# A two-stage ConvFFN: openings, stage change and round changes rewritten

## The chip, the core and the metric

One core of a Trainium2 chip runs the whole program. TensorE (PE) multiplies and writes to PSUM, VectorE (DVE) and ScalarE (ACT) work on PSUM and SBUF, GpSimd (POOL) on SBUF alone, and SyncE (SP) issues nearly all DMAs. Each engine takes its instructions in order from its own queue and waits on semaphores that others raise. The metric is the device time of one launch in microseconds, the median of the runs.

## The reference, cut to what matters

A two-layer trunk (D = 1024, hidden size 3072) for a prompt of 1024 tokens and 64 sample tokens, 1088 columns in all. Every layer has a mixer and, after it, a gated ConvFFN. The change touches the two ConvFFNs alone:

```
def conv_ffn(xn, buf, w_g, w_u, w_c, b_c, w_d):
    g = xn @ w_g
    gc, new_buf = causal_dwconv(g, buf, w_c, b_c)       # 3 taps over the tokens
    return (jax.nn.gelu(gc) * (xn @ w_u)) @ w_d, new_buf
# in the layer: y = y + conv_ffn(rmsnorm(y, g_ffn[l]), ...)
```

## The kernel before

Activations lie as feature rows by token columns: `x_residual` has 8 tiles of 128 features by 1088 columns. Products are of fp32 values split in two: a *high* part (a rounded copy, by ScalarE) and a *low* part (value minus high, by VectorE or GpSimd), and three matmuls stand for one: high by high, low weight by high, high weight by low (L2151). The third of them, which alone reads the lows of the tokens, is the last third of a product (L2144).

The ConvFFN (class `Ffn`, L1843) uses a seven-product block scheme on halves of depth, features and tokens. A **job** is seven products, numbers 0 to 6: B21, B11, T1, T2, B22, NT4, T3 (L1839). T1, T2, NT4 and T3 are sums of half tiles of the tokens; S1 to S4 are sums of weights, made by VectorE in PSUM. Three pairs of PSUM banks, d, a and bb, take the products in turn (`GROUPS`, L1848); some products add into a pair or overwrite it, and what it held must have been read first. In the first stage a product is 24 matmuls of 272 columns, in the second 18.

First stage: 24 jobs (`JOBS1`) in 12 pairs of a gate and an up job. ScalarE copies products 0, 2, 3 and 5 out (`copy_out`), VectorE adds 1, 4 and 6 (`add_out`). In each pair the gate is scaled by the root of the squares (`scale_gate`), convolved (`conv_first` on ScalarE, `conv_tap` and `conv_samples` on VectorE), put through gelu, scaled again by GpSimd (`gate_scale`) and multiplied with up (`hidden_tile`); its four sums are made (`hidden_sum`) and SyncE stores it to DRAM. Second stage: 16 jobs in four **rounds** of four. In a round a quarter of the hidden features, seven *pieces* fetched from DRAM to staging buffers and made high by `piece_hi` and low by `piece_lo`, is multiplied with four groups of weights, and VectorE adds each product to the residual (`add_residual`). The residual was spilled to DRAM for the first stage and is fetched back (`reload`).

The order on each engine is written out by hand: `opening` (PE), `opening_act`, `open_dve` and `opening_dve` for job 0; then the loops in `tensor`, `scalar`, `vector`, `gpsimd` and `sync`; `down_first` is VectorE's order in the second stage's first job. The norm is applied late: GpSimd sums the squares of the tiles (L1661), a product with ones sums over features (L1669), ScalarE makes Ln and Exp of it (L1676, L1679), all inside job 0. Residual tiles 6 and 7 come last out of the mixer's output projection (`Output`, L1747), whose evacuations (L1828) stand in VectorE's queue among the opening's first steps.

In a round's first job TensorE waits before each product for the piece's low:

```
                    if m % QUARTERS == 0:
                        pe.wait_ge(*self.x_lo_done(m // QUARTERS, i))
```

## Time and profile before

| | us |
|---|---|
| median of 3 runs | 2579.86 (2578.29 to 2581.73) |
| profiled execution, its time | 2576.1 |
| its span | 2574.4 |
| first opening, first product to job 2's product 3 | 637.6 to 705.7 |
| second opening, the same | 1758.2 to 1828.9 |
| stage changes: the second stage's first two jobs | 1158.8 to 1205.9, 2282.0 to 2329.5 |
| round changes | three in each ConvFFN, the first at 1238 |

In a row of a timeline the first number is the start in us from the span's start, the second the length; then engine, line of the kernel, operation, what is written and read, shape, and the number of instructions merged. In brackets stands how long the engine was idle before it, and who ended that. Matmuls overlap, so the row of a product is a little longer than its share.

### The profile page before, as it was taken

The numbers are of one execution on the slowest core, as the hardware profiler recorded it, in microseconds if no ns is written. First come the engines' busy times: TensorE is split into PE (matmuls) and PEld (weight loads), VectorE is DVE, ScalarE is ACT, GpSimd is POOL, SyncE is SP. The second block draws the span as 40 slices with busy tenths as digits, with TensorE's granted clock in tenths as the row PEclk, the third lists the DMA queues.
The fourth block names the chain that finished last, engine by engine and source line by source line (L and its number), as shares of the span: only waits on it lengthen the run. The fifth ranks groups of instructions, "written<-read, shape, count | busy, mean of one in ns | idle before, by whom it ended". The sixth has DMA issues, their size and how long they took to land.

```text
span 2574.4 us, 46180 instructions
## 1 busy us (share of the span) xinstructions
PE 2466.7 (96%) x18693; PEld 2364.2 (92%) x18693; DVE 1765.6 (69%) x2158; ACT 1148.4 (45%) x1851; POOL 961.9 (37%) x623
## 2 busy tenths in 40 slices
PE   8999998899899999998999999998999999989998
PEld 7888886689899999998999999998999999989998
DVE  7466557645877777777778444637878777787775
ACT  5565756533544444442334433424444444443331
POOL 3234333214445454542223411343545454532221
PEclk9999999999999999999999999998999999999999
DMA  5101106752222232336443211222232222265422
GB/s 183 52 27 51 44 26 217 262 190 77 88 98 103 89 111 80 111 113 243 140 141 93 56 40 37 58 68 90 92 110 86 106 93 98 90 232 199 139 89 82
DMA packets 214178, 276.99 MB, mean 108 GB/s; under 512 B 11438, under 2 KB 158999, under 8 KB 210895
## 3 DMA queue, kind: packets, MB, share of 16 engines
q1 hardware_dynamic: 212910, 271.83, 31.7%
q8 instruction: 149, 2.44, 0.4%
q10 hardware_dynamic: 576, 2.10, 0.2%
q14 instruction: 63, 0.51, 0.1%
q0 software_dynamic: 480, 0.11, 0.0%
HBM read 203.57 MB, written 70.43 MB: 106 GB/s over the span
## 4 chain that ended last, share of the span: by engine, by line
PE 64%; DVE 9%; issue 3%; ACT 1%; POOL 1%; DMA 1%; SPq 0%; DVEq 0%; ACTq 0%; POOLq 0%
PE psum_all L2153 52%; PE psum_all L2810 7%; PE psum_all L148 3%; DVE down_x_ffn L2106 2%; DVE psum_all L2091 1%; DVE x_residual L2519 1%; DVE x_residual L2470 1%; DMA w_raw<-in_w_gate_dram 1%; PE psum_all L2862 0%; PE psum_all L2826 0%; POOL rms_scale L1661 0%; DVE blocks_down L2095 0%; POOL w_lo_part L113 0%; DVE ffn_x_sums L2407 0%; PE psum_all L2850 0%
## 5 line engine op out<-in xcount | busy, mean ns | idle before, releaser
L2153 PE MATMUL psum_all<-ffn_x,blocks 128*128 128x272 f32 x5760 | 737.6, 289 | 22.6 <-DVE ffn_x L2416 13.8
L2153 PEld LDWEIGHTS psum_all<-ffn_x,blocks 128*128 128x128 f32 x5760 | 731.0, 190 | 24.3 <-issue 15.7
L2153 PE MATMUL psum_all<-down_x_ffn,blocks_down 128*128 128x272 f32 x2880 | 376.9, 292 | 24.4 <-DVE x_residual L2519 11.5
L2153 PEld LDWEIGHTS psum_all<-down_x_ffn,blocks_down 128*128 128x128 f32 x2880 | 370.3, 191 | 28.7 <-issue 27.9
L2268 ACT COPY x_residual<-psum_all 128x544 f32<-128x544 f32 x192 | 117.9, 614 | 374.7 <-PE psum_all L2153 371.3
L113 POOL TENSOR_TENSOR w_lo_part<-w_raw,w_hi_part 128x1024 fp32r<-128x1024 f32 x52 | 126.8, 2439 | 355.9 <-ACT w_hi_part L97 355.8
L2519 DVE TENSOR_TENSOR x_residual<-x_residual,psum_all 128x544 f32<-128x544 f32 (+1 forms) x224 | 178.4, 797 | 114.2 <-PE psum_all L2153 112.7
L2470 DVE SCALAR_TENSOR_TENSOR x_residual<-x_residual,ffn_params 128x1088 f32<-128x1088 f32 x96 | 215.2, 2242 | 0.0
L2101 POOL TENSOR_TENSOR x_residual<-x_residual,rms_scale 128x1088 f32<-128x1088 f32 x48 | 153.2, 3191 | 151.7 <-ACT x_residual L2297 151.7
L2455 DVE TENSOR_TENSOR x_residual<-x_residual,psum_all 128x544 f32<-128x544 f32 x144 | 130.1, 904 | 93.2 <-PE psum_all L2153 91.3
L2095 DVE TENSOR_TENSOR blocks<-psum_all,blocks 128x512 fp32r<-128x512 f32 x144 | 99.2, 689 | 121.8 <-ACT blocks L2249 121.8
L2810 PE MATMUL psum_all<-operand_a,w_hi_part 128*128 128x364 f32 (+1 forms) x672 | 170.0, 331 | 0.0
L909 PE MATMUL psum_all<-in_hi_even,w_hi_part 128*128 128x384 f32 (+1 forms) x456 | 157.0, 344 | 1.1 <-DVE xb_padded L1430 0.6
L1363 POOL TENSOR_TENSOR take_then_weights<-take_then_weights,x_residual 128x511 f32<-128x511 f32 (+3 forms) x96 | 94.9, 999 | 158.0 <-DVE x_residual L1395 119.1
L2153 PE MATMUL psum_all<-ffn_x,block_a 128*128 128x272 f32 x1152 | 152.0, 288 | 1.3 <-ACT rms_scale L1676 1.3
L2153 PE MATMUL psum_all<-ffn_x,block_s 128*128 128x272 f32 x1152 | 151.8, 287 | 0.0
L909 PE MATMUL psum_all<-in_lo_even,w_hi_part 128*128 128x384 f32 (+1 forms) x456 | 149.3, 327 | 0.0
L2153 PEld LDWEIGHTS psum_all<-ffn_x,block_a 128*128 128x128 f32 x1152 | 146.9, 188 | 2.4 <-issue 2.4
L909 PE MATMUL psum_all<-in_hi_even,w_lo_part 128*128 128x384 f32 (+1 forms) x456 | 149.1, 327 | 0.0
L2153 PEld LDWEIGHTS psum_all<-ffn_x,block_s 128*128 128x128 f32 x1152 | 147.0, 188 | 0.0
L1395 DVE TENSOR_TENSOR_SCAN x_residual<-x_residual,all_ones 128x512 f32<-128x512 f32 (+3 forms) x96 | 91.8, 990 | 73.1 <-ACT x_residual L1183 73.1
L2500 POOL TENSOR_TENSOR x_residual<-x_residual 128x544 f32<-128x544 f32 x88 | 130.1, 1479 | 6.3
(361 smaller groups left out, 4630.1 us busy)
## 6 DMA issues: line engine op xcount, KB each, us to landing
staging_ffn<-hidden_spill SPq DMA_DIRECT2D x54, 816.0 KB, 5.2
hidden_spill<-x_residual SPq DMA_DIRECT2D x24, 1088.0 KB, 4.0
w_raw<-in_w_gate_dram SPq DMA_DIRECT2D x24, 1024.0 KB, 5.4
x_residual<-in_w_up_dram SPq DMA_DIRECT2D x24, 1024.0 KB, 5.2
pages<-in_cache_k_dram SPq DMA_DIRECT2D x64, 256.0 KB, 3.7
pages<-in_cache_v_dram SPq DMA_DIRECT2D x64, 256.0 KB, 4.6
x_spill<-x_residual SPq DMA_DIRECT2D x24, 546.0 KB, 5.4
x_residual<-x_spill SPq DMA_DIRECT2D x24, 546.0 KB, 5.8
```

The lines of the kernel that those rows point to most:

```text
L113: pool.tensor_tensor(dst if dst is not None else self.lo[:, par, :], self.raw[:, par, :], (hi if hi is not None else self.hi[:, par, :]).b ...
L909: mm = pe.matmul(bank(key, 0, b - a), wt[:, n % 2, col], xt[:, k, a:b], start=k == 0 and s == 0, stop=k == KT - 1 and s == 2)
L1363: pool.tensor_tensor(t[:, 0:n - 1], t[:, 0:n - 1], k[:, 1:n], ALU.mult).then_inc(weighted, 1)
L2095: eng.tensor_tensor(self.block(n, i, 1).rearrange("p (q c) -> p q c", c=P), self.source(n, i), self.block(n, i, 0).bitcast(F32).rearrange( ...
L2101: pool.tensor_tensor(self.conv[:, r, :], self.conv[:, r, :], self.core.rb[:, 0:USED], ALU.mult).then_inc(self.gr_ready, 1)
L2153: mm = pe.matmul(self.core.ps[:, b + h, 0:HB], wt[:, q * P:(q + 1) * P], xt[:, q, HB * h:HB * (h + 1)], start=first and at == 0, stop=at = ...
L2268: act.copy(self.half(self.target(n, r), h).rearrange("p (h n) -> p h n", h=2), self.group(name)).then_inc(self.act_out, 1)
L2455: dve.tensor_tensor(dst, dst, src, ALU.add).then_inc(self.dve_out, 1)
L2470: o.did(dve.scalar_tensor_tensor(gc, gb[:, j:j + USED], par[:, f + FT * j:f + FT * j + 1], gc, ALU.mult, ALU.add))
L2500: eng.tensor_tensor(dst, x, y, op).then_inc(self.hsum, 1)
L2519: dve.tensor_tensor(dst, dst, src, ALU.add).then_inc(self.dve_out, 1)
L2810: mm = pe.matmul(self.core.ps[:, self.lane_bank(f), 0:width(c)], wm[:, is_u, col], xm[:, k, chunk(c)], start=k == 0 and s == 0, stop=k == ...
```

## The change

All of it is in `Ffn` and in what calls it:

- Opening: TensorE's order in job 0 is 1, 2, 0, 4, 3, 5, 6 (it was 1, 0, 2, 3, 4, 5, 6). Each of the four token sums has one low, whole, by VectorE (`sum_lo`); GpSimd made half of two of them. TensorE waits for such a low at the product's last third (`made_first`). VectorE evacuates tile 6 behind S1 and S2 alone, the other first weights come after it.
- The squares of tiles 6 and 7 go to another scratch (`late_sq`), so that the high of block 4 waits for less. Squares are addressed as two halves. GpSimd's last addition of squares, the sums over features, Ln and Exp come in job 1.
- VectorE's order in job 1 is `first_pair_dve`. The last steps of the first pair (gelu 1, both gate scalings, `hidden_tile(0)`, the hidden sums) come in job 2.
- Spill and reload share one semaphore for each pair of tiles, and waits ask for the pair that they need.
- Stage change: ScalarE makes the highs of two pieces behind product 4 of job 23, of one behind each of 5 and 6, of three in job 24 (all seven came in job 23); the last gelu comes behind the copy of product 5, GpSimd's last gate scaling in job 24; VectorE has a new order in `down_first`; in the first ConvFFN SyncE asks for piece 4 ahead of the reload.
- Round changes: TensorE waits for a piece's high before the product and for its low at its last third. T1's low moves on VectorE from behind product 4's add to behind product 5's.
- The transposes of the state rows stand behind product 3 of job 25, not 2.

```
+    FIRST_PIECES = {(-1, 4): (B21, B11), (-1, 5): (T1,), (-1, 6): (T2,), (0, 1): (NT4,), (0, 2): (T3,)}
...
-                if up and i in (3, 5):
+                if n == 0 and i == 1:
+                    self.add_squares(pool, KT - 1)
+                if up and n > 1 and (i == 3 or i == 5 and n < JOBS1 - 1):
                     self.gate_scale(pool, t, (i - 3) // 2)
-                if up and i == 6 and n < JOBS1 - 1:
-                    self.hidden_sum(pool, t, T1)
-                if n and n % 2 == 0 and n < JOBS1 and i == 0:
+                elif n == JOBS1 and i == 1:
+                    self.gate_scale(pool, PAIRS - 1, 1)
+                elif n == 2 and i in (0, 1):
+                    self.gate_scale(pool, 0, i)
+                if up and i == 6 and 1 < n < JOBS1 - 1 or n == 2 and i == 1:
+                    self.hidden_sum(pool, (n - 1) // 2, T1)
+                if n and n % 2 == 0 and n < JOBS1 and i == (1 if n == 2 else 0):
                     for k in (T3, T2, NT4):
                         self.hidden_sum(pool, t - 1, k)
             if behind and n >= JOBS - QUARTERS:
                 behind(n - (JOBS - QUARTERS))
...
+            if x_low and (q, s) == (0, 2):
+                x_low()
...
     def opening(self, pe):
+        def made_first(i):
+            pe.wait_ge(*self.lo_ready(0, i))
+            pe.wait_ge(self.act_lead, self.T_HI[i])
+            self.multiply(pe, 0, i, lambda: pe.wait_ge(self.lead_lo, self.T_LO[i]))
         pe.wait_ge(self.out.evac, KT - 1)
         pe.wait_ge(self.b_lo, 10)
         pe.wait_ge(*self.lo_ready(0, 1))
         self.multiply(pe, 0, 1)
-
-        def tile_ready(q):
-            if q == 3:
-                pe.wait_ge(self.b_lo, 11)
-
         pe.wait_ge(self.out.evac, KT)
-        self.multiply(pe, 0, 0, tile_ready)
-        pe.wait_ge(*self.lo_ready(0, 2))
-        pe.wait_ge(self.t1_lo, 2)
-        self.multiply(pe, 0, 2)
-        pe.wait_ge(*self.lo_ready(0, 3))
-        pe.wait_ge(self.t2_lo, 1)
+        made_first(T1)
+        pe.wait_ge(self.b_lo, 11)
+        pe.wait_ge(*self.lo_ready(0, 0))
+        self.multiply(pe, 0, 0)
+        pe.wait_ge(self.b_lo, 12)
+        pe.wait_ge(*self.lo_ready(0, 4))
+        pe.wait_ge(self.act_out, 1)
+        self.multiply(pe, 0, 4)
         pe.wait_ge(self.dve_out, 1)
-        self.multiply(pe, 0, 3)
-        pe.wait_ge(self.act_out, 1)
-        self.sums_pe(pe, (0, 1))
-        pe.wait_ge(*self.lo_ready(0, 4))
-        pe.wait_ge(self.b_lo, 12)
+        made_first(T2)
         pe.wait_ge(self.act_out, 2)
-        self.multiply(pe, 0, 4)
-        self.sums_pe(pe, (2,))
-        pe.wait_ge(*self.lo_ready(0, 5))
-        pe.wait_ge(self.t2_lo, 2)
-        pe.wait_ge(self.s_root, 3)
-        self.multiply(pe, 0, 5)
-        pe.wait_ge(*self.lo_ready(0, 6))
-        pe.wait_ge(self.t3_lo, 2)
+        made_first(NT4)
         pe.wait_ge(self.act_out, 3)
-        self.multiply(pe, 0, 6)
+        made_first(T3)
 
     def tensor(self, pe, before=None, behind=None):
...
                     if m % QUARTERS == 0:
-                        pe.wait_ge(*self.x_lo_done(m // QUARTERS, i))
+                        pe.wait_ge(self.x_hi, 7 * (m // QUARTERS) + i + 1)
...
+                low = None
+                if m >= 0 and m % QUARTERS == 0:
+                    low = lambda: pe.wait_ge(*self.x_lo_done(m // QUARTERS, i))
+                self.multiply(pe, n, i, low)
+                if n == 1 and i == 1:
+                    pe.wait_ge(self.act_out, 5)
+                    self.sums_pe(pe, (0, 1))
+                elif n == 1 and i == 3:
+                    self.sums_pe(pe, (2,))
+                if m == 1 and i == 3:
                     pe.wait_ge(self.dve_out, dve + 1)
                     self.turn_state_rows(pe)
...
     def opening_act(self, act):
...
+        for i in range(3):
+        self.tile_hi(act, KT - 2)
+        self.block_hi(act, 0, 3)
+            self.even_copy(act, T1, q, 0)
+        act.wait_ge(self.s_sum, KT - 3)
+        self.block_hi(act, 0, 4)
+        self.even_copy(act, T3, 0, 1)
+        self.even_copy(act, T3, 1, 1)
+        self.sum_hi(act, T1)
+        self.even_copy(act, T3, 2, 1)
+        self.even_copy(act, T3, 3, 1)
+        self.square(act, KT - 2)
+        self.tile_hi(act, KT - 1)
+        self.square(act, KT - 1)
+        self.copy_out(act, 0, 2)
+        self.sum_hi(act, T2)
+        self.sum_hi(act, NT4)
+        self.sum_hi(act, T3)
+        self.block_hi(act, 1, 0)
+        self.block_hi(act, 1, 1)
+        self.copy_out(act, 0, 5)
+        for i in range(2, 7):
...
+    def first_conv_act(self, act, i):
+        if i == 1:
+            self.roots_act(act, (0, 1))
+        elif i == 3:
+            self.roots_act(act, (2,))
+            self.conv_first(act, 0, 0)
+            self.conv_first(act, 0, 1)
+        elif i == 6:
+            self.gelu(act, 0, 0)
...
+                if (n, i) == (JOBS1, 0):
+                    self.piece_hi(act, 0, B22)
...
+                elif (n, i) == (2, 0):
+                    self.gelu(act, 0, 1)
+                elif n == JOBS1 - 1 and i == 3:
+                    self.gelu(act, t, 0)
+                if n in (JOBS1 - 1, JOBS1):
+                    for k in self.FIRST_PIECES.get((n - JOBS1, i), ()):
+                        self.piece_hi(act, 0, k)
                 elif n >= JOBS1 and p == QUARTERS - 1 and r < ROUNDS - 1:
                     self.piece_hi(act, r + 1, i)
-                if m == 1 and i == 2:
+                if (n, i) == (JOBS1 - 1, 5):
+                    self.gelu(act, t, 1)
+                if m == 1 and i == 3:
...
+    def sum_lo(self, dve, i):
+        dve.wait_ge(self.act_lead, self.T_HI[i])
+        if i != T1:
+            dve.wait_ge(self.sum_lead, self.T_MADE[NT4][3])
+        dve.tensor_tensor(self.operand(0, i, 1), self.temp(i), self.operand(0, i, 0).bitcast(F32), ALU.subtract
+                          ).then_inc(self.lead_lo, 1)
...
+    def open_dve(self, dve):
+        self.tile_dve(dve, KT - 2)
+            self.t1_sum(dve, q)
+        self.t3_sum(dve, 0)
+        self.t3_sum(dve, 1)
+        self.t2_sum(dve, 0)
+        self.block_lo(dve, 0, 4)
+        self.sum_lo(dve, T1)
+    def opening_dve(self, dve):
+        self.nt4_sum(dve, 0)
+        self.tile_lo(dve, KT - 1, 0, B21, 0)
+        self.t3_sum(dve, 2)
+        self.t3_sum(dve, 3)
+        self.tile_lo(dve, KT - 1, 1, B22, 1)
+        for q in (1, 2, 3):
+        for q in (1, 2, 3):
+            self.nt4_sum(dve, q)
+        self.sum_lo(dve, T2)
+        self.sum_lo(dve, NT4)
+        self.add_out(dve, 0, 4)
+        self.sum_lo(dve, T3)
+        self.add_out(dve, 0, 6)
+    def first_pair_dve(self, dve, o):
+        self.block_lo(dve, 1, 4)
+        self.add_out(dve, 1, 1)
+        self.block_lo(dve, 1, 6)
+        self.block_sum(dve, 2, "S1")
+        self.block_sum(dve, 2, "S2")
+        self.block_lo(dve, 2, 2)
+        self.block_sum(dve, 2, "S4")
+        self.block_lo(dve, 2, 3)
+        self.block_sum(dve, 2, "S3")
+        self.scale_dve(dve)
+        self.scale_gate(dve, 0, 0)
+        self.scale_gate(dve, 0, 1)
+        self.conv_tap(dve, o, 0, 0, 1)
+        self.add_out(dve, 1, 4)
+        self.conv_tap(dve, o, 0, 0, 0)
+        self.conv_samples(dve, o, 0, 0)
+        self.block_lo(dve, 2, 4)
+        self.conv_tap(dve, o, 0, 1, 1)
+        self.conv_tap(dve, o, 0, 1, 0)
+        self.conv_samples(dve, o, 0, 1)
+        self.add_out(dve, 1, 6)
+        self.block_lo(dve, 2, 6)
...
+            self.block_sum(dve, u, "S1")
+            self.block_sum(dve, u, "S2")
+            if t == 1:
+                self.hidden_tile(dve, 0, 0)
+            self.hidden_tile(dve, t - 1, 1)
+            self.add_out(dve, g, 1)
+            self.block_lo(dve, u, 2)
+            self.block_sum(dve, u, "S4")
...
-                if turn and i == 4:
+                if turn and i == 5:
                     self.piece_lo(dve, r + 1, T1)
...
         self.piece_lo(dve, 0, T1)
+        self.block_lo(dve, n, 6)
         self.add_residual(dve, n, 0)
+        self.piece_lo(dve, 0, T2)
         self.add_residual(dve, n, 1)
-        self.piece_lo(dve, 0, T2)
+        self.next_sums(dve, n + 1)
         self.piece_lo(dve, 0, B22)
         self.add_residual(dve, n, 2)
+        self.next_lo(dve, n + 1, 2)
         self.piece_lo(dve, 0, NT4)
         self.add_residual(dve, n, 3)
+        self.next_lo(dve, n + 1, 3)
         self.piece_lo(dve, 0, T3)
-        self.next_sums(dve, n + 1)
-        self.next_lo(dve, n + 1, 2)
         self.add_residual(dve, n, 4)
-        self.next_lo(dve, n + 1, 3)
         self.add_residual(dve, n, 5)
         self.next_lo(dve, n + 1, 4)
```

## Rows read from the trace of the kernel before

**Rows 1.** The profile's page, busy time of each engine

```profile
PE 2466.7 (96%) x18693; PEld 2364.2 (92%) x18693; DVE 1765.6 (69%) x2158; ACT 1148.4 (45%) x1851; POOL 961.9 (37%) x623
```

**Rows 2.** Who TensorE waited for: us in total, times, longest us

```profile
PE psum_all L2153 <- DVE ffn_x L2416: 13.8, 2, 8.2
...
PE psum_all L2153 <- DVE x_residual L2519: 11.5, 8, 3.6
...
PE psum_all L2153 <- DVE down_x_ffn L2106: 9.4, 10, 4.0
```

**Rows 3.** Timeline of TensorE, opening of the first ConvFFN

```profile
637.60 3.18 PE L2153 MATMUL psum_all<-ffn_x,blocks 128*128 128x272 f32 x24
...
643.47 6.40 PE L2153 MATMUL psum_all<-ffn_x,blocks 128*128 128x272 f32 x48 [2.69 <-DVE x_residual L1828]
...
658.09 5.47 PE L2153 MATMUL psum_all<-ffn_x,blocks 128*128 128x272 f32 x24 [8.23 <-DVE ffn_x L2416]
...
699.69 12.24 PE L2153 MATMUL psum_all<-ffn_x,blocks 128*128 128x272 f32 x96 [0.41 <-DVE x_residual L2455]
```

**Rows 4.** Windows: length, busy us of five queues, TensorE's granted clock, DMA share, GB/s

```profile
658.00:660.00 2.00, 1.91 (x8) 1.94 (x9) 2.00 (x3) 1.17 (x1) 0.75 (x1) 0.50 0.24 74
```

**Rows 5.** Timeline of TensorE, opening of the second ConvFFN

```profile
1766.31 9.00 PE L2153 MATMUL psum_all<-ffn_x,blocks 128*128 128x272 f32 x48 [4.91 <-DVE x_residual L1828]
...
1822.89 12.25 PE L2153 MATMUL psum_all<-ffn_x,blocks 128*128 128x272 f32 x96 [0.72 <-DVE x_residual L2455]
```

**Rows 6.** Timeline of VectorE, first opening: sums of half tiles, a low

```profile
637.96 2.16 DVE L2387 SCALAR_TENSOR_TENSOR ffn_x_sums<-x_residual,params,ffn_x_sums 128x544 f32<-128x544 f32 x3
...
646.38 3.05 DVE L2387 SCALAR_TENSOR_TENSOR ffn_x_sums<-x_residual,params,ffn_x_sums 128x544 f32<-128x544 f32 x1
...
655.58 2.42 DVE L2416 TENSOR_TENSOR ffn_x<-ffn_x_sums,ffn_x 128x2176 fp32r<-128x2176 f32 x1
```

**Rows 7.** Timeline of VectorE, first opening: a scaling and a tap of 1088 columns

```profile
676.54 1.28 DVE L2461 TENSOR_TENSOR x_residual<-x_residual,rms_scale 128x1088 f32<-128x1088 f32 x1
...
681.90 1.34 DVE L2470 SCALAR_TENSOR_TENSOR x_residual<-x_residual,ffn_params 128x1088 f32<-128x1088 f32 x1
```

**Rows 8.** Timeline of VectorE, steady state, the add of a job's product 6

```profile
1095.97 1.29 DVE L2455 TENSOR_TENSOR x_residual<-x_residual,psum_all 128x1088 f32<-128x1088 f32 x1 [3.43 <-PE psum_all L2153]
```

**Rows 9.** Timeline of GpSimd: adding squares, a weight low, a gate scaling

```profile
646.17 2.68 POOL L1661 TENSOR_TENSOR rms_scale<-rms_scale,square_scratch 128x1088 f32<-128x1088 f32 x1 [1.58 <-ACT square_scratch L1652]
...
679.54 1.29 POOL L2095 TENSOR_TENSOR blocks<-w_raw,blocks 128x512 fp32r<-128x512 f32 x1 [2.90 <-ACT blocks L2249]
...
1152.05 2.57 POOL L2101 TENSOR_TENSOR x_residual<-x_residual,rms_scale 128x1088 f32<-128x1088 f32 x1 [6.41 <-ACT x_residual L2297]
```

**Rows 10.** Timeline of ScalarE: Exp of the root, a weight high

```profile
668.93 1.11 ACT L1679 ACTIVATE rms_scale<-rms_scale 128x1088 f32<-128x1088 f32 x1
...
684.83 0.60 ACT L2249 ACTIVATE blocks<-psum_all 128x512 fp32r<-128x512 f32 x1
```

**Rows 11.** Timeline of TensorE, stage changes of both ConvFFNs

```profile
1169.26 9.60 PE L2153 MATMUL psum_all<-down_x_ffn,blocks_down 128*128 128x272 f32 x54 [4.00 <-DVE down_x_ffn L2106]
...
1196.80 4.74 PE L2153 MATMUL psum_all<-down_x_ffn,blocks_down 128*128 128x272 f32 x36
...
2307.66 8.54 PE L2153 MATMUL psum_all<-down_x_ffn,blocks_down 128*128 128x272 f32 x54 [3.60 <-DVE x_residual L2519]
```

**Rows 12.** Timeline of VectorE, first stage change

```profile
1166.79 0.56 DVE L2095 TENSOR_TENSOR block_s<-psum_all,block_s 128x384 fp32r<-128x384 f32 x1 [4.13 <-ACT block_s L2249]
```

**Rows 13.** Timeline of TensorE, first round change

```profile
1238.04 11.51 PE L2153 MATMUL psum_all<-down_x_ffn,blocks_down 128*128 128x272 f32 x90 [0.45 <-issue]
...
1252.35 2.50 PE L2153 MATMUL psum_all<-down_x_ffn,block_s 128*128 128x272 f32 x18 [0.54 <-DVE down_x_ffn L2106]
...
1255.83 11.57 PE L2153 MATMUL psum_all<-down_x_ffn,blocks_down 128*128 128x272 f32 x90 [0.98 <-DVE x_residual L2519]
```

**Rows 14.** Timeline of VectorE, first round change

```profile
1242.83 0.72 DVE L2519 TENSOR_TENSOR x_residual<-x_residual,psum_all 128x544 f32<-128x544 f32 x1 [0.63 <-PE psum_all L2153]
```

More of the change, by code:

```diff
@@ L132, in chunk, with halves @@
     return slice(c * CH, min((c + 1) * CH, USED))
+def halves(tile):
+    return tile.rearrange("p (h n) -> p h n", h=2)
 def width(c):
@@ L1660, in add_squares @@
             pool.wait_ge(self.s_sum, m - 1)
[L1661 to L1662 removed]
+        total = halves(self.core.rb[:, 0:USED])
+        pool.tensor_tensor(total, total, self.square_at(m), ALU.add).then_inc(self.s_sum, 1)
     def sums_pe(self, pe, which):
@@ L1670, in sums_pe, with roots_act @@
                       start=True, stop=True).then_inc(self.s_mm, 1)
-    def roots_act(self, act):
-        act.preload_act_table_set("natural_log_exp_and_others")
-        for c in range(3):
+    def roots_act(self, act, which=(0, 1, 2)):
+        if 0 in which:
+            act.preload_act_table_set("natural_log_exp_and_others")
+        for c in which:
             act.wait_ge(self.s_mm, c + 1)
@@ L1677, in roots_act @@
                            scale=1.0 / D, bias=EPS).then_inc(self.s_root, 1)
+        if 2 not in which:
+            return
         act.wait_ge(self.s_root, 3)
@@ L2144, in multiply @@
         order = [(q, s) for s in range(3) for q in range(depth)]
-        if ready:
-            order = [(q, s) for q in range(depth) for s in range(3)]
         mm = None
         for at, (q, s) in enumerate(order):
-            if ready and s == 0:
-                ready(q)
+            if x_low and (q, s) == (0, 2):
+                x_low()
             wt, xt = ((w_hi, x_hi), (w_lo, x_hi), (w_hi, x_lo))[s]
@@ L2255, in copy_out @@
         r, h, name = {0: (0, 0, "d"), 2: (1, 1, "bb"), 3: (0, 1, "a"), 5: (1, 0, "d")}[i]
-        act.wait_ge(self.product, max(self.done(n, k) for k in range(i + 1)))
+        act.wait_ge(self.product, self.done(n, i))
         if t:
@@ L2569, in vector @@
             self.add_out(dve, u, 6)
-            self.block_lo(dve, u + 1, 6)
+            if not last:
+                self.block_lo(dve, u + 1, 6)
         self.down_first(dve)
```

208 lines of the change are left out of this document (80 added, 128 removed).

## The prediction

> **What bounds the kernel now.** I read the page's busy line first, then who TensorE waits for, then TensorE's timeline where those waits lie, and last the other queues there. TensorE is busy 96% of the span [rows 1], so only its holes and its slow stretches can be won. The waits name three places [rows 2]: sums and lows of the first job of each ConvFFN (13.8 us), residual adds (11.5) and piece lows (9.4) of the second stage. All three wait for VectorE.
>
> Opening, first ConvFFN: product B11 starts at 637.60, the next only after the last tile's evacuation at 643.47, T1 at 658.09 after 8.23 us of nothing [rows 3]. T1's 24 matmuls then take 5.47 us where B11's take 3.18 (3.0 from start to start; below a product is 3.0 us): after that hole TensorE stands at a granted clock of 0.50, its 1.2 GHz level [rows 4]. From the first product to job 2's product 3 (two products behind the 699.69 row) it is 705.7 - 637.6 = 68.1 us. In the second ConvFFN the first product starts 4.91 + 3.2 before 1766.31, at 1758.2, and job 2's product 3 at 1822.89 + 6.0: 70.7 us [rows 5]. The ideal is 17 products, 51 us, plus the sums' 0.6.
>
> **The opening, rewritten.** Prices: a sum of a half tile 0.72 us (2.16 for three), a whole low (128x2176) 2.42, a two-input operation of 1088 columns 1.28, a convolution tap 1.34, the add of a whole tile from PSUM 1.29 [rows 6 to 8]. On a span in which GpSimd adds squares, one such half sum takes 3.05 [rows 6, 9]: the two serialise when VectorE reads two SBUF tensors.
>
> (The Trainium skill, GPSIMD Engine Reference, section Specifications, says that GpSimd's SBUF interfaces are shared with VectorE and that instructions with two SBUF inputs contend. The trace agrees. It speaks against moving all four lows to VectorE only where GpSimd still works beside them: without that sharing the sum would be some 2.5 us better per opening, by my entries marked * below.)
>
> - B11 now runs 0 to 3.0. VectorE comes off the T1 sums and T1's low (2.42) at +2.0 and evacuates the last tile (1.3) to +3.3: T1 starts at +3.4, 0.4 late. The old hole of 8.23 goes, as B21 and B22 stand between T1 and T2.
> - B21 and B22 follow without a hole, to +12.4. T2 needs VectorE's add of B11, which stands behind three T2 and three NT4 sums (4.3): 0.5 late. Its low is 0.35 late at the last third.
> - NT4 on time. T3's low runs beside GpSimd's last squares: 1.5* late. So the first job ends 23.8 after its start instead of 37.5 (and 39.8).
> - Job 1: product 1 waits for the last add of job 0, behind two block sums and a low: 0.9. The sums of squares (0.35) now stand inside job 1. Product 3 of job 1 ends at +37.0.
>
> What is late next is the root of the squares. It was ready before job 1 started; now Ln and Exp (1.11) follow job 1's product 3: ready at +39.9 [rows 10]. Behind it in VectorE's queue stand two scalings (2.5), the wait for ScalarE's first tap (0.2), four taps (5.1), two adds (1.9), six small sample operations (1.9), a low (0.6), and 1.0* for GpSimd's blocks: 13.2 us in a row. The add of job 1's product 6, for which job 2's product 1 waits, is done at +53.1; TensorE is there at +49.2. **New stall one: 3.9 us.**
>
> Stall two follows from the code. Job 2's product 3 needs the add of its product 1, and in VectorE's queue both hidden tiles of pair 0 now stand ahead of that add. The second needs GpSimd's gate scaling, which GpSimd issues behind low 1 of job 3, whose high ScalarE makes only when job 2's product 1 is done. So from that product's end: high 0.6, low 1.3, gate scaling 2.6, hidden tile 1.3, add 0.65 (half of 1.29), and 0.6 of hand-overs: 7.05 us, of which product 2 covers 3.0 [rows 7 to 10]. **4.0 us, in each ConvFFN.** Product 3 starts at 53.1 + 3.0 + 7.05 = +63.2. Against 68.1 and 70.7 that is 4.9 and 7.5 us won, 12.4 together.
>
> The clock: holes of 3.60, 4.00 and 4.91 us were followed by 1.2 GHz; 54 matmuls took 8.54 and 9.60 instead of 6.9, 48 took 9.00 instead of 6.0: 1.6 to 3.0 us lost; the hole of 2.69 cost nothing [rows 3, 5, 11]. I take 1.6 for each new stall of about 4 us, two per opening: -6.4. Bounds: 0 and 12. Opening: **6.0 us won** of both, bounds -3 and +28 (no stall, no fall).
>
> (The Trainium skill, TensorE: Matmul & The Clock Gate, section Why this matters for your kernels, asks to keep idle gaps between bursts short lest the clock halve. That speaks against a rewrite that trades one hole of 8 us for two of 4; by it all four stalls pay. The rows above say the same of holes from 3.60 on.)
>
> **Stage change.** Only two pieces, not four, stand ahead of ScalarE's copy of product 5: the 0.99 us in front of the down stage goes, but the next product waits until 1162.7 for an add behind two piece lows on VectorE, as now. From there VectorE sets the pace: between 1157 and 1195 it idles only 4.13 us, waiting for a block high that stood behind a piece's DMA [rows 12], and 0.8 in shorter gaps. The new order puts T1's low there and asks for piece 4 earlier; in the first ConvFFN SyncE's queue issues it ahead of the reload. These 4.9 us are the gain, up to 1196.80, where job 25's product 3 waits for the hidden sums. Against it: GpSimd's last gate scaling (2.57) moves from VectorE's idle time into its busy time, 1.0; the state rows' transposes (0.85) ran in the hole and now stand behind product 3; the hole before that product grows from about 2 to 4.3 and I charge 1.6 for the clock. 4.9 - 1.0 - 0.85 - 1.6 = 1.5 us. The second ConvFFN takes 0.4 longer there now and so wins 1.9. Bounds for both: -4 (clock at 2.7, piece DMAs late) and +9. **3.4 us.**
>
> **Round changes,** six. TensorE waits 0.45 + 0.54 + 0.98 us [rows 13]. The wait for a low at the last third takes away the 0.54, T1's low behind add 5 the 0.45. But VectorE idles only 0.63 us between 1226 and 1256 [rows 14], and the 0.98 is the end of its queue: what TensorE gains ahead it gives back there. Only those 0.63 can shrink: 0.6 each, **3.6 us.** Bounds 0 (all given back) and 11.8 (all 1.97 won). The wait itself is one more instruction in front of a matmul. No row has one inside a product; it can win nothing, and costs at most the 0.45 at 1238.04, which ends in such a wait. In the rounds VectorE's queue would cover it, so I take 0.
>
> Squares written through a view of two halves, the scratch in the ring, merged semaphores: same element counts; 0, hidden on ScalarE and GpSimd.
>
> **Sum.** 6.0 + 3.4 + 3.6 = 13.0 us. The profiled execution took 2576.1 us (span 2574.4), 3.8 below the runs' median 2579.86; against it the change makes 2563.1, against the median 2566.9: I say **2567**.
>
> **Rivals.**
> - The first pair is covered better than I count (VectorE's queue has less in it, or ScalarE frees it): stalls half as long, clock stays up. 2 x (4.0 + 3.2) = 14 us more: 2553. For it: VectorE's total work is the same and it was idle little in this stretch before. Against it: the chain through low 1 of job 3 is fixed by the order. 0.22.
> - The stalls cost more: each pays 2.7 us, VectorE is late in the stage change, the rounds give nothing: (12.4 - 10.8) + 0.5 + 0 = 2 us: 2578, no change to be seen. 0.15.
> - Slower: the backlog of 4 us which VectorE has at job 2 is handed from pair to pair. If each of the 11 pairs after it stalled another 1.0 us, that is 22 us in both ConvFFNs: 2589. It decides where VectorE's idle time in a pair is less than the backlog. Against it: in the steady state it idles 3.43 us in front of one add alone [rows 8], and about 8 in a pair. 0.07.
> - That low waits are moved without effect because VectorE is the bound is in the third term already; entirely so, it makes 2570.
>
> **How the numbers follow.** 0.56 for my case (2559 to 2574), 0.22, 0.15, 0.07. The range takes in the first rival down to 2551 and stops at 2577: about 0.2 outside. Within 0.2% (5.2 us: what a measurement of this kernel can tell from no change) is 2574.7 to 2585. Faster 0.79, same 0.14, slower 0.07.
>
> **What would show it.** After: first job some 24 us long, hole before T1 under 1 us; TensorE waiting 3 to 5 us for VectorE's add at job 2's product 1 and about 4 us at product 3, in both ConvFFNs, with 1.2 GHz behind them; one hole of about 4 us before job 25's product 3; one hole of 1.5 to 2 us per round change in place of three. I am wrong if the two stalls of job 2 are not there (then faster), if holes appear in job 4 and later (slower), or if a round change loses its 0.98.

## The result, and the profile after

The changed kernel takes **2594.31 us** (median of 4 runs, 2591.18 to 2595.35) where the kernel before took 2579.07 on the same chip (4 runs, 2576.43 to 2581.73): ratio 1.0053, 95% interval 1.0040 to 1.0065. It is **15 us slower**; I had said 12 us faster. The profiled execution has a span of 2591.8 us against 2574.4. The first product of the first ConvFFN starts at 641.16 there and at 637.60 before; in the 14 traces of this study that moment lies anywhere from 637.2 to 642.1, whatever was changed, so the 3.6 us by which the two traces differ there, of 17.4 between their spans, say nothing.

TensorE's waits, longest first (line 2538 is the add of an up-stage product, line 2602 the add of a down-stage product):

```profile
PE psum_all L2174 <- DVE x_residual L2538: 31.6, 9, 6.7
PE psum_all L2174 <- DVE x_residual L2602: 22.4, 10, 4.6
PE psum_all L2174 <- issue: 9.7, 6, 2.9
```

Against [rows 2] the waits for sums and piece lows are nearly gone (1.6 and 1.4 us are left of 13.8 and 9.4), and waits for VectorE's adds have taken their place: they went from one queue entry to another. The third row, "issue", is waits in the stage changes for which the view names nobody. TensorE's timeline of the first opening (start, us, idle before and who ended it in brackets):

```profile
641.16 6.20 PE L2174 MATMUL psum_all<-ffn_x,blocks 128*128 128x272 f32 x48
647.59 6.27 PE L2174 MATMUL psum_all<-ffn_x,blocks 128*128 128x272 f32 x48 [0.23 <-DVE ffn_x L2433]
655.14 3.61 PE L2174 MATMUL psum_all<-ffn_x,blocks 128*128 128x272 f32 x24 [1.28 <-DVE x_residual L2538]
664.52 1.27 PE L2174 MATMUL psum_all<-ffn_x,block_s 128*128 128x272 f32 x8 [0.77 <-DVE ffn_x L2462]
671.65 3.24 PE L2174 MATMUL psum_all<-ffn_x,blocks 128*128 128x272 f32 x24 [2.87 <-DVE x_residual L2538]
702.04 8.73 PE L2174 MATMUL psum_all<-ffn_x,blocks 128*128 128x272 f32 x48 [6.70 <-DVE x_residual L2538]
715.54 4.87 PE L2174 MATMUL psum_all<-ffn_x,blocks 128*128 128x272 f32 x20 [4.76 <-DVE x_residual L2538]
```

This answers [rows 3]. The hole of 8.23 us before T1 is gone, and the first job ends 24.5 us after its start. But job 1's product 1 waits 2.87, job 2's product 1 waits 6.70 (stall one) and its product 3 waits 4.76 (stall two). Product 3 of job 2 starts 715.54 - 641.16 = 74.4 us after the first product; before it was 68.1. In the second ConvFFN the same three holes stand, and product 3 comes at +74.25 against 70.7 [rows 5]:

```profile
1799.51 4.77 PE L2174 MATMUL psum_all<-ffn_x,blocks 128*128 128x272 f32 x24 [2.87 <-DVE x_residual L2538]
1830.80 7.69 PE L2174 MATMUL psum_all<-ffn_x,blocks 128*128 128x272 f32 x48 [6.69 <-DVE x_residual L2538]
1843.26 2.15 PE L2174 MATMUL psum_all<-ffn_x,blocks 128*128 128x272 f32 x8 [4.76 <-DVE x_residual L2538]
```

The 48 matmuls behind stall one take 8.73 and 7.69 us, those behind stall two 8.79 and 8.19 (their rows are cut short above), where such a row is 6.2 at full speed: 8.7 us over four stalls. Behind the hole of 2.87 us the 24 matmuls took 3.24 us in the first ConvFFN and 4.77 in the second. Granted clock by stretches of the first opening (PE busy, clock, DMA share, GB/s):

```profile
692.00:694.00 2.00, 2.00 (x18) 1.00 0.03 8
702.00:704.00 2.00, 1.96 (x9) 0.50 0.00 0
716.00:718.00 2.00, 2.00 (x11) 0.50 0.48 194
720.00:722.00 2.00, 2.00 (x13) 0.70 1.01 418
```

So TensorE stands at its 1.2 GHz level (0.50) behind each of the two stalls. Between job 2 and the stage change only one hole is left, of 0.40 us, in the second ConvFFN. From the first product to the end of the up stage the traces of before give 521.2 and 523.8 us (the two ConvFFNs), those of after 530.0 and 529.9: **14.9 us of the loss lie in the openings and first pairs.** The stage changes, from the end of the up stage to job 26's start, went from 47.1 and 47.5 to 45.9 and 46.9: 1.8 us won. The round changes:

```profile
1266.44 13.04 PE L2174 MATMUL psum_all<-down_x_ffn,blocks_down 128*128 128x272 f32 x90 [1.92 <-DVE x_residual L2602]
1333.27 11.51 PE L2174 MATMUL psum_all<-down_x_ffn,blocks_down 128*128 128x272 f32 x90 [1.96 <-DVE x_residual L2602]
1398.66 11.51 PE L2174 MATMUL psum_all<-down_x_ffn,blocks_down 128*128 128x272 f32 x90 [2.06 <-DVE x_residual L2602]
2395.74 13.08 PE L2174 MATMUL psum_all<-down_x_ffn,blocks_down 128*128 128x272 f32 x90 [2.42 <-DVE x_residual L2602]
```

One hole stands where three stood [rows 13], and it is as long as the three together: 2.07 us on average of six against 1.93. From hole to hole an undisturbed round is shorter all the same: 1398.66 - 1333.27 = 65.4 us, where two of before are 66.0 apart (1255.83 in [rows 13], and 1321.83). But behind two of the six holes 90 matmuls took 13.04 and 13.08 us instead of 11.5, which takes 3.1 us back. From job 26 to the end of the stage the two traces differ by 0.3 us won in the first ConvFFN and 1.0 lost in the second.

### The profile page after: what moved, and what is told of

Same layout as the page of the kernel before. It is cut to its first block, busy times and chain, and to the rows that moved or that the text cites. A ratio compares the mean times of both kernels' runs of the same rounds, so it can differ in the third digit from the quotient of the medians.

```text
span 2591.8 us, 46196 instructions
## 1 busy us (share of the span) xinstructions
PE 2470.2 (95%) x18693; PEld 2368.0 (91%) x18693; DVE 1771.8 (68%) x2158; ACT 1147.8 (44%) x1849; POOL 945.0 (36%) x619
## 4 chain that ended last, share of the span: by engine, by line
PE 66%; DVE 8%; issue 2%; ACT 1%; POOL 1%; DMA 0%; DVEq 0%; ACTq 0%; POOLq 0%
PE psum_all L2174 51%; PE psum_all L2892 7%; PE psum_all L153 6%; DVE down_x_ffn L2130 2%; DVE psum_all L2115 1%; DVE x_residual L2602 1%; DVE ffn_x L2462 1%; PE psum_all L2944 0%; PE psum_all L2908 0%; POOL x_residual L2125 0%; DVE blocks_down L2119 0%; DVE x_residual L2538 0%; DMA staging_ffn<-hidden_spill 0%; PE psum_all L2932 0%; DVE x_residual L2583 0%
```

## The experiments

My theory after this reading: VectorE's queue order in the first pair makes stall one, a chain through GpSimd's gate scaling makes stall two, and the clock falls behind each; the second stage is about neutral. The rival: waits inside a product and one long hole in place of three short ones cost the time. All times are medians, all ratios are to the kernel before on the same chip. The experiments ran on three chips, on which the kernel before took 2580.8, 2577.6 and 2579.1 us, so runs of different chips are compared by their ratios; 0.0010 is 2.6 us. The last column is read from one trace each, for the first and the second ConvFFN.

| kernel | us | ratio, 95% | first product to end of up stage |
|---|---|---|---|
| before | 2579.1 | | 521.2, 523.8 |
| after | 2594.3 | 1.0053 (1.0040-1.0065) | 530.0, 529.9 |
| second stage only | 2576.4 | 0.9983 (0.9974-0.9992) | 522.7, 523.7 |
| same, low waits at the head | 2575.7 | 0.9991 (0.9982-0.9999) | 524.0, 523.4 |
| after, low waits at the head | 2591.6 | 1.0052 (1.0039-1.0066) | 529.2, 531.9 |
| after, busy stalls | 2584.1 | 1.0008 (0.9999-1.0017) | 527.2, 526.6 |
| after, add of job 1 first | 2588.5 | 1.0025 (1.0013-1.0036) | 527.8, 526.9 |
| after, hidden tiles late | 2599.3 | 1.0069 (1.0055-1.0083) | 534.8, 533.5 |
| after, add before hidden tile 1 | 2585.5 | 1.0025 (1.0015-1.0035) | 525.7, 527.2 |
| after, gate scaling later | 2594.0 | 1.0055 (1.0042-1.0069) | 531.1, 530.4 |
| after, root early | 2584.7 | 1.0029 (1.0020-1.0039) | 525.3, 527.9 |
| first pair reordered | 2575.7 | 0.9994 (0.9985-1.0003) | 519.5, 523.1 |
| first pair, again | 2558.7 | 0.9918 (0.9906-0.9931) | 512.4, 513.3 |
| the last, low waits at the head | 2554.6 | 0.9904 (0.9891-0.9917) | 512.3, 513.2 |

**Second stage only.** The kernel before with the change's stage-change and round-change edits (pieces, SyncE's order, `down_first`, `x_low`, T1's low behind add 5), the opening untouched.

> The kernel before with the change's second-stage parts alone: order of the first pieces and of VectorE's queue at the stage change, the wait for a token low at a product's last third, T1's low behind add 5 at the round changes. The opening is as before. Theory (the whole loss is in the openings and first pairs; stage changes win 1 to 2 us in all, round changes about nothing): 2578 us (2575 to 2580). My forecast's own terms for these parts (3.4 + 3.6 us won): 2572. Rival (waits inside a product, or one hole of 2 us in place of three small ones with the clock falling behind it, are what costs): 2584 or more.

Measured 2576.4, 4.4 us under before on that chip (interval 2 to 7). The rival falls: the second stage does not cost the time. The opening's edits cost the whole loss and more: by the ratios, 1.0053 against 0.9983, 18 us.

**Busy stalls.**
```
+    if n == 2: self.idle_work(pe, "bb", 50)   # i == 1
+    if n == 2: self.idle_work(pe, "d", 36)    # i == 3
```
(Each stands behind a wait for the last reader of its PSUM banks, and ahead of the wait that makes the stall.)

> The changed kernel, but TensorE multiplies into a free PSUM group while it waits in stall one (50 matmuls of 272 columns, 6.3 us) and in stall two (36, 4.5 us); the waits themselves stay. Nothing but the clock is changed. Theory (each slow stretch behind a stall costs 1.4 to 2.8 us more than the stall itself): products 1 and 2 take 3.0 us each instead of 4.4, stall two ends 1.4 us sooner, products 3 and 4 gain 2.7: 4.2 us per ConvFFN, 2586 us (2583 to 2589). Rival (the clock is a minor matter, under 1 us in all, or the extra matmuls delay the real ones): 2593 or more.

```profile
704.66 6.27 PE L2174 MATMUL psum_all<-ffn_x,blocks 128*128 128x272 f32 x48 [0.44 <-DVE x_residual L2550]
710.77 4.68 PE L2180 MATMUL psum_all<-ffn_x,blocks 128*128 128x272 f32 x36
715.69 6.26 PE L2174 MATMUL psum_all<-ffn_x,blocks 128*128 128x272 f32 x48 [0.25 <-DVE x_residual L2550]
```

TensorE runs its useless matmuls (line 2180) through each stall, and the 48 behind stall one take 6.27 instead of 8.73. 2584.1, ratio 1.0008 against 1.0053: 10 to 12 of the fifteen us are the clock's. The trace of the change has 8.7 us behind the four stalls. The third hole of each opening (2.87 us) was not filled here. Behind it this execution took 5.78 and 4.77 us for 24 matmuls, so its product 3 of job 2 still comes at +74.1 and +72.9.

**Add of job 1 first.**
```
         self.block_lo(dve, 2, 4)
+        self.add_out(dve, 1, 6)
         self.conv_tap(dve, o, 0, 1, 1)
...
-        self.add_out(dve, 1, 6)
```


> The changed kernel with one line moved: VectorE adds job 1's product 6 right behind the first half of the convolution instead of behind the second. Theory (VectorE's queue behind the late root makes stall one, the chain through GpSimd's gate scaling makes stall two, and the two overlap): stall one goes from 6.7 to under 0.5 us, but stall two grows to some 8 to 10, since the second gelu still waits for the end of the convolution; job 2's product 3 comes 4 to 5 us earlier in each ConvFFN: 2585 us (2582 to 2588). Rival A (each stall has its own cause, so the first vanishes whole and the second stays 4.8): 2578. Rival B (the loss is not in the first pair): 2594, no change.

```profile
712.64 8.42 PE L2174 MATMUL psum_all<-ffn_x,blocks 128*128 128x272 f32 x48 [10.03 <-DVE x_residual L2538]
```

Stall one is gone (no hole at job 2's product 1), and stall two is 10.03 in place of 4.76: of 6.7 us taken out, 5.3 came back. 2588.5, ratio 1.0025: 7 us less than the change, where I expected 9. Rival A, two independent stalls, falls.

**Hidden tiles late.** Both hidden tiles of pair 0 moved behind `block_sum(dve, u, "S3")` of job 3.

> The changed kernel with pair 0's two hidden tiles moved behind VectorE's add of job 2's product 1 (and the block work after it). Theory: stall two (4.8 us at job 2's product 3) goes whole, stall one (6.7) stays; with the second hole goes most of one slow stretch of TensorE (2.7 us): 7.5 us per ConvFFN, 2579 us (2577 to 2585). Rival A (VectorE is the bound there, the hidden tiles only hold up something later, such as job 3's copies out): under 2 us each, 2590 or more. Rival B (the loss is not in the first pair): 2594.

A miss: 2599.3. Stall two went, as foretold, and a new one of 7.31 us stood in job 3, since ScalarE waited for the store of the hidden sums, VectorE for ScalarE (8.37 us) and TensorE for VectorE:

```profile
700.43 13.62 PE L2174 MATMUL psum_all<-ffn_x,blocks 128*128 128x272 f32 x96 [6.69 <-DVE x_residual L2538]
736.36 8.38 PE L2174 MATMUL psum_all<-ffn_x,blocks 128*128 128x272 f32 x48 [7.31 <-DVE x_residual L2538]
727.49 1.30 ACT L2315 ACTIVATE x_residual<-x_residual,ffn_params 128x1088 f32<-128x1088 f32 x1 [9.25 <-DMA hidden_spill<-x_residual]
```

The first two rows are TensorE's, the third is ScalarE's start of pair 1's convolution, behind a wait of 9.25 us for that DMA. The hidden tiles have a deadline of their own.

**Add before hidden tile 1.**
```
             self.hidden_tile(dve, 0, 0)
+            self.add_out(dve, g, 1)
             self.hidden_tile(dve, t - 1, 1)
-            self.add_out(dve, g, 1)
```


> The changed kernel with VectorE's add of job 2's product 1 put between pair 0's two hidden tiles instead of behind both; the second hidden tile comes 0.7 us later at most. The run with both tiles some 6 us later lost stall two and then stood 7.3 us in job 3, where ScalarE waited for the store of the hidden sums. Theory (stall two is only the order of these two operations; the later stall was the store's): stall two (4.8 us) goes, nothing of over 1 us appears behind it, and one slow stretch of 2.7 us goes with it: 7.5 us per ConvFFN, 2579 us (2577 to 2584). Rival (the store of the hidden sums holds ScalarE in any order in which TensorE is 4.8 us earlier): the time comes back as a hole in job 3, 2590 or more.

```profile
705.04 14.15 PE L2174 MATMUL psum_all<-ffn_x,blocks 128*128 128x272 f32 x96 [6.69 <-DVE x_residual L2538]
735.65 6.24 PE L2174 MATMUL psum_all<-ffn_x,blocks 128*128 128x272 f32 x48 [1.46 <-DVE x_residual L2538]
```

Swapping two operations takes stall two away; 1.46 us (2.54 in the second ConvFFN) comes back in job 3. 2585.5, between theory (2579) and rival (2590); by the ratios 7 us less than the change, where I expected 15.

**Gate scaling later.** GpSimd's `gate_scale(pool, 0, 0)` moved from behind block low 0 to behind block low 1 of job 3.

> The changed kernel, but GpSimd scales both halves of pair 0's gate behind job 3's block low 1, so nothing large runs on GpSimd beside VectorE's convolution and its six sample operations. Theory (these small operations took 1.11 and 2.43 us instead of 0.3 because GpSimd was reading and writing SBUF; my 1.0 for it was 3 too small): stall one shrinks from 6.7 to about 3.7, and stall two grows by the 2.5 us of the first scaling: about 0.5 us per ConvFFN in all, 2593 us (2590 to 2595). Rival (the operations are late for another reason): stall one stays 6.7 and the time rises by 5: 2599.

VectorE's small sample operations (64 columns), of after first, then of this kernel:

```profile
691.80 1.32 DVE L2566 SCALAR_TENSOR_TENSOR x_residual<-gate_sample,ffn_params,x_residual 128x64 f32<-128x64 f32 x1
696.80 1.11 DVE L2564 TENSOR_SCALAR x_residual<-gate_sample,ffn_params 128x64 f32<-128x64 f32 x1
697.95 2.43 DVE L2566 SCALAR_TENSOR_TENSOR x_residual<-gate_sample,ffn_params,x_residual 128x64 f32<-128x64 f32 x1
700.41 0.28 DVE L2568 SCALAR_TENSOR_TENSOR x_residual<-gate_sample,ffn_params,x_residual 128x64 f32<-128x64 f32 x1
```
```profile
698.50 1.13 DVE L2565 TENSOR_SCALAR x_residual<-gate_sample,ffn_params 128x64 f32<-128x64 f32 x1
699.66 0.28 DVE L2567 SCALAR_TENSOR_TENSOR x_residual<-gate_sample,ffn_params,x_residual 128x64 f32<-128x64 f32 x1
701.61 7.58 PE L2175 MATMUL psum_all<-ffn_x,blocks 128*128 128x272 f32 x48 [4.55 <-DVE x_residual L2539]
716.32 8.65 PE L2175 MATMUL psum_all<-ffn_x,blocks 128*128 128x272 f32 x48 [7.13 <-DVE x_residual L2539]
```

The same operation takes 0.28 us instead of 2.43 once the gate scaling isn't beside it; stall one is 2.15 shorter, stall two 2.4 longer, the sum nearly unchanged (11.7 for 11.5), as expected, and so is the time, 2594.0. Stall one shrank less than the 3 us that I expected. What GpSimd was doing in after:

```profile
696.60 1.26 POOL L2119 TENSOR_TENSOR blocks<-x_residual,blocks 128x512 fp32r<-128x512 f32 x1 [3.56 <-ACT blocks L2271]
697.82 2.47 POOL L2125 TENSOR_TENSOR x_residual<-x_residual,rms_scale 128x1088 f32<-128x1088 f32 x1
```

VectorE's rows end where these end (697.91 and 697.86; 700.38 and 700.29): each small operation ended 0.1 us behind GpSimd's instruction. In the second kernel GpSimd's low still runs beside the first of them, which takes 1.13 us.

**Low waits at the head.** `low()` called in front of `self.multiply(pe, n, i)` in the second stage; once on after, once on the kernel with the second stage only.

> The changed kernel, but in the second stage TensorE's wait for a token low stands in front of the product again, not at its last third; all orders stay as changed. If the wait at the last third hides the end of a low (up to one third of a product, 0.75 us, in each of six round changes and at two places of each stage change), this is slower by 3 to 6 us: 2597 to 2600. If VectorE's queue bounds the round change whatever TensorE does (the reading by which I forecast 0.6 us a round), it is 2594 to 2595. If waiting inside a product itself costs, it is faster: under 2592.

> The kernel before with the second-stage orders of the change, but with its own waits in front of the products (no wait inside a product). It differs from the run with all second-stage parts (0.9983) by that wait alone. Theory (the orders win what is won there, the wait inside the product wins no idle time and loses clock): 3 to 4 us below it, 0.9970 of before, 2572 us. Rival (the wait at the last third is what won the 4.4 us): at or above the kernel before, 2579.

1.0052 against 1.0053, and 0.9991 against 0.9983: with and without the wait inside the product no difference in total can be told. In the trace each round change of the first has holes of about 0.8 and 1.0 us, and never a slow stretch in its six:

```profile
1326.73 2.50 PE L2174 MATMUL psum_all<-down_x_ffn,block_s 128*128 128x272 f32 x18 [0.85 <-DVE down_x_ffn L2130]
1330.22 11.52 PE L2174 MATMUL psum_all<-down_x_ffn,blocks_down 128*128 128x272 f32 x90 [0.99 <-DVE x_residual L2604]
...
1395.53 11.51 PE L2174 MATMUL psum_all<-down_x_ffn,blocks_down 128*128 128x272 f32 x90 [0.98 <-DVE x_residual L2604]
```

From 1330.22 to 1395.53 are 65.3 us. So a round is 0.6 us shorter than before also with the wait at the head: the 0.6 come from VectorE's order (T1's low behind add 5), not from where TensorE waits. My reading that VectorE's queue bounds the round stands. What the place of the wait changes is the slow stretch. Behind the one long hole (1.5 to 2.4 us) 23 of the 60 round changes in ten traces have it, at 1.5 us each; with the waits at the head none of 18 has. From job 26 to the end of the stage the two ConvFFNs are 3.0 to 3.8 us shorter with the waits at the head, in each of the three pairs of kernels; the totals of the two pairs here do not show it. My expectation of 2572 for the second run was not met (2575.7).

**Root early.** The add of job 0's product 6 directly behind block sum S1, the last sum of squares and root behind job 1's product 2, VectorE's scalings ahead of block low 3.

> Of the same edits only those ahead of the convolution: the add of job 0's product 6 directly behind the first block sum, and the last root behind job 1's product 2 with the scalings at once behind it. Theory: the hole of 2.9 us before job 1's product 1 goes, the root is ready some 6 us earlier, but stall one only shrinks from 6.7 to about 4 (TensorE comes 2.9 us earlier too) and stall two stays 4.8: 5.4 us per ConvFFN, 2583 us (2580 to 2587). Rival (the root's time does not matter, since VectorE's queue is full in any case): only the 2.9 per ConvFFN, 2588 or more.

Measured 2584.7: stall one fell to 2.6, more than the 4 I expected, and stall two stayed 4.76. (The view names GpSimd's low as the releaser of the first; it ended 0.1 us behind VectorE's add.)

```profile
696.25 7.59 PE L2174 MATMUL psum_all<-ffn_x,blocks 128*128 128x272 f32 x48 [2.59 <-POOL blocks L2119]
708.61 8.15 PE L2174 MATMUL psum_all<-ffn_x,blocks 128*128 128x272 f32 x48 [4.76 <-DVE x_residual L2539]
```

**First pair reordered**, and **again**: the edits of root early with the moves below; the lines marked "again" are in the second kernel alone.
```
 # VectorE, pair 0
 self.conv_tap(dve, o, 0, 1, 1)
+self.add_out(dve, 1, 6)
 self.conv_tap(dve, o, 0, 1, 0)
 self.block_lo(dve, 2, 6)
+self.block_sum(dve, 3, "S1")      # again
+self.block_sum(dve, 3, "S2")      # again
+self.add_out(dve, 2, 1)           # again
 self.conv_samples(dve, o, 0, 1)
...
 # hidden tiles: 0 ahead of, 1 behind block low 2 and S4 of job 3
 # ScalarE: gelu(0, 1) at (2, 1) instead of (2, 0)
 # again: copy_out(1, 0) ahead of block_hi(1, 3..6);
 #        conv_first(1, 0) at (3, 0) instead of (2, 5)
```


> The changed kernel with the first pair ordered anew: the add of job 0's product 6 directly behind the first block sum; the last sum of squares and its root behind job 1's product 2 instead of 3, and VectorE's scalings at once behind it; the adds of job 1's product 6 and of job 2's product 1 inside and directly behind the convolution; the second gelu one step later; the hidden tiles behind that add. Theory (job 0's new order is sound and VectorE's order in the first pair is what costs): no hole of more than 1.5 us between the first job and job 4; from the first product to job 2's product 3 some 56 us instead of 74.4, and one or both slow stretches gone: 18 to 22 us per ConvFFN, less up to 4 for the store of the hidden sums: 2556 us (2550 to 2566), 20 below the kernel before. Rival (VectorE has about 60 us of work in that stretch, so order can't help below that and the backlog comes back as holes in jobs 2 to 4): 2572 or more.

```profile
673.18 2.46 PE L1677 MATMUL psum_all<-rms_scale,all_ones 128*128 128x364 f32 x4 [2.83 <-ACT x_residual L2292]
703.46 7.77 PE L2174 MATMUL psum_all<-ffn_x,blocks 128*128 128x272 f32 x48 [2.15 <-DVE x_residual L2539]
```

2575.7, not the 2556 expected: job 2's product 3 comes at +64.0, not +56. The 2.87 us at job 1's product 1 had only moved one place on, to the sums of squares, since ScalarE's copy of product 0 stood behind four block highs; and VectorE's add behind the samples was 2.15 late. In the second ConvFFN another hole of 2.12 us stood in job 3. Three more moves in two queues:

> The reordered first pair, with what its own trace shows as next: ScalarE copies job 1's product 0 out ahead of four block highs (TensorE waited 2.8 us for it in front of the sums of squares), VectorE adds job 2's product 1 ahead of the six sample operations of the second half (2.15 us), and ScalarE starts pair 1's convolution one step later, so that it doesn't wait for the store of the hidden sums. Theory (order in VectorE's and ScalarE's queues is still what costs there): from the first product to job 2's product 3 59 us instead of 64.0, and the slow stretch of 1.5 us behind it gone: 6 us per ConvFFN, 2563 us (2559 to 2569). Rival (VectorE's 60 us of work in that stretch are now the bound; the time comes back in jobs 2 to 4): 2571 or more.

```profile
674.98 0.84 PE L1677 MATMUL psum_all<-rms_scale,all_ones 128*128 128x360 f32 x2 [1.02 <-ACT rms_scale L1685]
687.74 15.62 PE L2174 MATMUL psum_all<-ffn_x,blocks 128*128 128x272 f32 x120
734.21 10.99 PE L2174 MATMUL psum_all<-ffn_x,blocks 128*128 128x272 f32 x86 [0.72 <-DVE x_residual L2544]
```

Now 120 matmuls of job 2 run without a hole; its product 3 starts three products behind 687.74, at +58.3. VectorE is busy 53.7 of these 58.3 us; in after it was busy 60.0 of 74.4. 2558.7: the rival (60 us of VectorE's work in that stretch are a bound) falls. Of the 6.3 us less, 3.7 are the two hidden tiles, which now stand behind product 3, and 1.0 the shorter waits of the sample operations for GpSimd (4.7 us for the six instead of 5.7). The moved work did not come back as holes: the next one, in job 4, is 0.72 us.

> The kernel of the run just described, with the second stage's low waits in front of the product. In the profile of the run with them there, each round change had holes of 0.8 and 1.0 us and full speed behind them, where the wait at the last third makes one of about 2.0, in two of six with TensorE slow behind it (90 matmuls in 13.04 us instead of 11.5). Theory (the split is worth only the clock): 3 to 5 us less than the kernel without it, 2559 us. Rival (nothing): the same time as that kernel within 1 us.

2554.6, the fastest of the study: ratio 0.9904 (0.9891 to 0.9917), **24 us below the kernel before and, by the ratios, 38 below the change.** Its interval overlaps that of the kernel with the wait inside the product (0.9918, 0.9906 to 0.9931), so the last 4 us are not shown to be the wait's by the totals; in the two traces the part from job 26 on is 3.0 us shorter.

## Why the prediction was wrong

**Failed first: the opening's arrival at job 2** ("job 2's product 3 starts at +63.2"; it was +74.4). The mechanism was right, both stalls stand where I put them and wait for what I named; the terms were too small. From the first opening's traces:
- The root, forecast for +39.9, was ready at +44.2. 0.7 us of it is the first job (24.5 for 23.8). 2.0 is "product 1 waits for the last add of job 0 ... 0.9": it was 2.87, since the block sum in front of that add ran beside GpSimd's last squares and took 3.03 us instead of 0.7, as the first two rows below show (VectorE's, then GpSimd's; compare [rows 6, 9]). I had counted that pairing for T3's low alone, and two block sums ahead of that add where the code has three. The rest, 1.6, is the sums of squares and the products around them (10.9 us from job 1's product 1 to the end of product 3, for 9.35).
- "13.2 us in a row" behind the root was 16.4. The six sample operations took 5.7 us in place of 1.9 + 1.0*: the gate-scaling run shows for the largest of them (2.43) that it was GpSimd's instruction that it waited for; the 1.32 and 1.11 end with GpSimd's lows.
- Stall two: 13.5 us from product 1's start to product 3's, forecast 10.05. 2.6 is product 1 itself at 1.2 GHz: ScalarE's high, which waits for it, starts 5.8 us after it (third row below) where a product is 3.0 and its row 3.2. 1.1 is the second hidden tile (2.40, beside GpSimd's hidden sum), and the hand-overs were 0.2 shorter than forecast. In the second ConvFFN product 1 cost 1.5 us too much in the same way. This part is the clock's, which I had charged as a term of its own.

```profile
664.39 3.03 DVE L2115 TENSOR_TENSOR psum_all<-x_residual 128x512 f32<-128x512 f32 x1
662.15 4.71 POOL L1670 TENSOR_TENSOR rms_scale<-rms_scale,square_scratch_in_ring 128x1088 f32<-128x1088 f32 x1
707.86 0.63 ACT L2271 ACTIVATE blocks<-x_residual 128x512 fp32r<-128x512 f32 x1 [6.01 <-PE psum_all L2174]
```

4.3 + 3.2 + 3.5 = 11.0 of the 11.2 us. Up to product 3 the openings cost 6.3 and 3.6 us where I had them win 4.9 and 7.5. Of these 22 us between forecast and trace 4 are product 1 at the low clock; nearly all the rest is waiting for VectorE.

**Failed second: "I take 1.6 for each new stall of about 4 us."** The traces have 2.2 each, 8.7 us. With TensorE kept busy the four stalls cost 10 to 12 us less, 2.5 to 2.9 each, near the upper end (12) that I had for all four. The stalls were also longer, 6.7 and 4.8. (The Trainium skill, TensorE: Matmul & The Clock Gate, section Why this matters for your kernels: keep idle gaps short. The busy-stall run agrees with the rule, at 10 to 12 us; in this case holes of 1.9 to 2.9 us had 1.2 GHz behind them too, though not each time.) (The page GPSIMD Engine Reference, section Specifications, of the Trainium skill has the sharing of SBUF interfaces that I cited; the trace agrees, and the wait lasted to the end of GpSimd's instruction, whatever the length of VectorE's.)

**Rounds, "0.6 each, 3.6 us":** the 0.6 was right for an undisturbed round of the first ConvFFN (66.0 to 65.4). The wait inside the product wins no idle time, as foretold; not foreseen were the slow stretches behind the merged hole, 3.1 us in this execution, so that by the traces 0.7 us was lost. **Stage change, "3.4 us":** 1.8 by the traces; the hole of 4.63 before job 25's product 3 and the slow 18 matmuls behind it (4.02 us for 2.4) are as foretold:

```profile
1205.76 4.02 PE L2174 MATMUL psum_all<-down_x_ffn,blocks_down 128*128 128x272 f32 x18 [4.63 <-DVE x_residual L2602]
```

The two together were 7.0 by forecast and 4.4 (2 to 7) by the run with them alone: in bounds.

**The rival on the other side** gave the right sign for a wrong reason: nothing was handed from pair to pair. I gave 0.07 to slower, because I took errors in the two stalls as errors of a few tenths in single rows; but both stalls are ends of chains in which every pairing with GpSimd adds, and each carries a fall of the clock with it.

Not tried: the change's new order of job 0 with the old order of the first pair. That job 0's new order is sound rests on its trace (24.5 us in place of 37.5) and on the last two kernels, which keep it.

## What to carry to other kernels

Closing one long hole brings TensorE early to every later consumer; before counting it, follow the next adds, copies, roots and stores through each queue, and look for the one whose place was chosen for the old arrival. Where VectorE reads SBUF alone beside a GpSimd operation, price it up to the end of GpSimd's, even the smallest, and price each stall with its clock. When the first reorder moves a hole one place on, look at the new releaser: here three further moves in two queues were worth 17 us (20 by the ratios), more than the whole change had lost.

## What was not expected of the hardware

A VectorE operation of 64 columns that reads SBUF takes 0.28 us alone and 2.43 us beside a GpSimd operation of 1088 columns, ending 0.1 us after it. The trace of before already had this, and I had priced these operations without looking at it: there the six took 4.8 us, and one of them 2.34, ending with GpSimd's gate scaling:

```profile
691.89 2.34 DVE L2481 TENSOR_SCALAR x_residual<-gate_sample,ffn_params 128x64 f32<-128x64 f32 x1
691.16 3.02 POOL L2101 TENSOR_TENSOR x_residual<-x_residual,rms_scale 128x1088 f32<-128x1088 f32 x1 [6.76 <-ACT x_residual L2297]
```

VectorE's add of a product, which reads PSUM and SBUF, did not wait. In the trace of "again" it took its usual 0.71 us in the middle of such a gate scaling:

```profile
693.43 3.01 POOL L2125 TENSOR_TENSOR x_residual<-x_residual,rms_scale 128x1088 f32<-128x1088 f32 x1
694.67 0.71 DVE L2544 TENSOR_TENSOR x_residual<-x_residual,psum_all 128x544 f32<-128x544 f32 x1
```

Behind holes of about 2 us TensorE's clock went either way, and the length of the hole alone did not decide it: behind 1.92 and 2.42 us it ran 90 matmuls in 13.0 us, behind 1.96, 2.06 and 2.31 at full speed, in one execution. Of the 60 merged holes, the 23 with a slow stretch behind them were 1.84 to 2.42 us long, the 37 without one 1.51 to 2.31. Two holes of up to 1.2 and 1.0 us, a product apart, never slowed it, in the eighteen round changes of the three kernels with the waits at the head.
